# Four hybrid layers on one core: the matmul stream takes a chunk's high part first, and tiles are placed at multiples of 512 bytes

## What is computed

```python
def layer_even(x, norm_g, w_in, w_out):            # layer_odd has the same frame
    h = rmsnorm(x, norm_g)
    qa, ka, va, iq, ik, iw, qb, kb, vb, gate = split_cols(h @ w_in, SPLIT0)
    ...                                             # sparse attention, dilated attention
    return x + (y * jax.nn.silu(gate)) @ w_out

def second_block(x, ...):
    h = rms_norm(x, norm_w[i]); proj = h @ w_in[i]
    o_a = gdn_branch(...)                           # gated delta rule, chunks of 64, triangular inverse
    o_b = rwkv7_branch(...)                         # RWKV-7 recurrence
    o_c = s5_branch(...)                            # complex diagonal scan, then a gelu and a product with glu_w
    branch_proj = einsum('blnc,ncd->blnd', stack([o_a, o_b, o_c]), w_branch[i])
    merged = sum(sigmoid(gate_logits + gate_b) * branch_proj)
    x = x + merged @ w_out[i]
    return rms_norm(x, final_norm_w)
```

## Time and profile before

| | us |
|---|---|
| runs | 2404.01, 2408.6, 2412.79 |
| profiled execution | 2403.41 |
| its span | 2401.6 |
| TensorE matmul busy | 2238.3 (93%) |
| VectorE busy | 1585.6 (66%) |
| ScalarE busy | 1070.5 (45%) |
| mean granted clock | 0.981 |

### The profile page before, as it was taken

The page is one execution under the profiler, slowest core; times in us unless marked ns, Lnnn a source line. Parts: engine busy times, 40 slices in busy tenths (PEclk is TensorE's granted clock), DMA queues, the critical chain, the costliest instruction groups (busy, mean ns, idle before and its releaser), DMA issues.

```text
span 2401.6 us, 35278 instructions
## 1 busy us (share of the span) xinstructions
PE 2238.3 (93%) x14268; PEld 1840.7 (77%) x14268; DVE 1585.6 (66%) x2362; ACT 1070.5 (45%) x1490; POOL 115.2 (5%) x188
## 2 busy tenths in 40 slices
PE   7999889999999999999999989888899989989997
PEld 6889678887878788877777767776677777767876
DVE  5665675558894546659999675665955556567754
ACT  5444565445444655553333653233444323244443
POOL 0000001010001001000000100001010000011000
PEclk9999999999999999999999999999999999989999
DMA  7666338667687449775554734249676333477753
GB/s 232 189 192 203 99 117 298 225 193 247 234 290 283 154 155 334 239 254 195 185 189 152 249 111 155 84 135 338 231 288 217 125 109 114 139 275 237 244 188 124
DMA packets 222594, 481.67 MB, mean 201 GB/s; under 512 B 14880, under 2 KB 51536, under 8 KB 217696
## 3 DMA queue, kind: packets, MB, share of 16 engines
q1 hardware_dynamic: 200112, 372.91, 47.2%
q0 software_dynamic: 22320, 106.51, 12.1%
HBM read 421.97 MB, written 57.40 MB: 200 GB/s over the span
## 4 chain that ended last, share of the span: by engine, by line
PE 72%; DVE 14%; DMA 6%; ACT 4%; issue 3%; POOL 0%; SPq 0%; ACTq 0%; POOLq 0%; DVEq 0%
PE mm_acc L291 59%; DVE mm_lo L208 3%; DMA mm_raw<-in_w_in 2%; ACT mm_hi L201 2%; PE s_bu L2819 1%; PE s_y L2832 1%; DMA rwk_src<-rw_rh 1%; DVE gdn_cv L1829 1%; DMA in_xt<-proj 1%; PE in_turn L374 1%; PE rwk_bank L2343 0%; DMA in_xt<-x 0%; DMA in_xt<-in_x 0%; DMA rw_v<-rwp_ft 0%; DVE s5t_tab L2718 0%
## 5 line engine op out<-in xcount | busy, mean ns | idle before, releaser
L208 DVE TENSOR_TENSOR mm_lo<-mm_raw,mm_hi 128x1024 fp32r<-128x1024 f32 (+4 forms) x672 | 791.9, 1185 | 525.6 <-ACT mm_hi L201 516.3
L201 ACT CAST mm_hi<-mm_raw 128x1024 fp32r<-128x1024 f32 (+4 forms) x672 | 681.8, 1019 | 862.2 <-PE mm_acc L291 827.2
L291 PE MATMUL mm_acc<-mm_hi,mm_aT_hi 128*128 128x512 f32 (+5 forms) x2208 | 880.3, 399 | 40.7 <-DVE mm_lo L208 35.5
L291 PE MATMUL mm_acc<-mm_hi,mm_aT_lo 128*128 128x512 f32 (+5 forms) x2208 | 852.0, 386 | 0.0
L291 PE MATMUL mm_acc<-mm_lo,mm_aT_hi 128*128 128x512 f32 (+5 forms) x2208 | 851.3, 386 | 0.0
L291 PEld LDWEIGHTS mm_acc<-mm_hi,mm_aT_hi 128*128 128x128 f32 x2208 | 421.6, 191 | 134.5 <-DVE mm_lo L208 48.0
L291 PEld LDWEIGHTS mm_acc<-mm_hi,mm_aT_lo 128*128 128x128 f32 x2208 | 420.8, 191 | 77.5
L291 PEld LDWEIGHTS mm_acc<-mm_lo,mm_aT_hi 128*128 128x128 f32 x2208 | 422.0, 191 | 67.5 <-issue 1.0
L291 PE MATMUL mm_acc<-mm_hi,in_yT_hi 128*128 128x512 f32 x256 | 101.7, 397 | 3.0 <-DVE mm_lo L208 3.0
L291 PE MATMUL mm_acc<-mm_hi,in_yT_lo 128*128 128x512 f32 x256 | 100.5, 393 | 0.0
L291 PE MATMUL mm_acc<-mm_lo,in_yT_hi 128*128 128x512 f32 x256 | 100.4, 392 | 0.0
(11 more groups left out here) (635 smaller groups left out, 2155.6 us busy)
## 6 DMA issues: line engine op xcount, KB each, us to landing
mm_raw<-in_w_in SPq DMA_DIRECT2D x384, 512.0 KB, 5.4
mm_raw<-in_w_out SPq DMA_DIRECT2D x96, 512.0 KB, 5.2
mm_raw<-in_w_in SPq DMA_DIRECT2D x72, 464.0 KB, 4.1
mm_raw<-in_w_branch SPq DMA_DIRECT2D x48, 512.0 KB, 5.3
proj<-mm_stage SPq DMA_DIRECT2D x46, 512.0 KB, 3.1
mm_raw<-in_w_in SPq DMA_DIRECT2D x32, 416.0 KB, 4.9
home_tab<-s5t_tab POOLq DMA_DIRECT2D x4, 2048.0 KB, 9.6
s_tab<-home_tab POOLq DMA_DIRECT2D x8, 1024.0 KB, 5.9
```

The source lines that it names most:

```text
L201: self.nc.scalar.copy(self.hi[:, c % RING, :, 0:t.w], self.raw[:, c % RAW, :, 0:t.w]).then_inc(self.hi_done, 1)
L208: self.nc.vector.tensor_tensor(self.lo[:, c % RING, :, 0:t.w], self.raw[:, c % RAW, :, 0:t.w], self.hi[:, c % RING, :, 0:t.w].bitcast(F32) ...
L291: last = nc.tensor.matmul(self.acc[s][m][:, 0:t.w], t.aT[a][:, k, m * P:(m + 1) * P], b[:, c % RING, k - k0, 0:t.w], start=(k == 0 and fir ...
```

## The change

Two edits. The first splits the wait of a chunk: TensorE waits for the high part, issues the 8 matmuls with `mm_hi`, then waits for the low part and issues the 4 matmuls with `mm_lo`. The second changes the allocation: a tile of under 512 bytes for each partition comes from the right end of SBUF, every other one starts at a multiple of 512 bytes. (`n` counts 4 bytes an element.)

```diff
+LINE = 512
...
     def sb(self, name, shape, dt=F32):
-        return self.stack.enter_context(self.nc.sbuf_tensor(f"{self.name}_{name}", shape, dt))
+        n = 4 * int(np.prod(shape[1:]))
+        place = dict(side="right") if n < LINE else dict(align_bytes=LINE)
+        return self.stack.enter_context(self.nc.sbuf_tensor(f"{self.name}_{name}", shape, dt, **place))
...
+            pe.wait_ge(self.hi_done, c + 1)
+            for k in range(k0, k0 + KC):
+                for m in range(MT):
+                    for a in range(2):
+                        nc.tensor.matmul(self.acc[s][m][:, 0:t.w], t.aT[a][:, k, m * P:(m + 1) * P], self.hi[:, c % RING, k - k0, 0:t.w],
+                                         start=(k == 0 and a == 0), stop=False)
             pe.wait_ge(self.lo_done, c + 1)
             for k in range(k0, k0 + KC):
                 for m in range(MT):
-                    for a, b, first, end in ((0, self.hi, True, False), (0, self.lo, False, False), (1, self.hi, False, True)):
-                        last = nc.tensor.matmul(self.acc[s][m][:, 0:t.w], t.aT[a][:, k, m * P:(m + 1) * P],
-                                                b[:, c % RING, k - k0, 0:t.w],
-                                                start=(k == 0 and first), stop=(k == t.KT - 1 and end))
+                    last = nc.tensor.matmul(self.acc[s][m][:, 0:t.w], t.aT[0][:, k, m * P:(m + 1) * P], self.lo[:, c % RING, k - k0, 0:t.w],
+                                            start=False, stop=(k == t.KT - 1))
             last.then_inc(self.used, 1)
```

## The result

| | before | after |
|---|---|---|
| median of six runs, us | 2408.98 (2404.01 to 2412.79) | 2387.4 (2381.28 to 2394.58) |
| ratio | | 0.9909, interval 0.9895 to 0.9923 |
| profiled execution, us | 2403.41 | 2388.49 |
| its span | 2401.6 | 2386.7 |

The kernel became faster by 0.91% (21.9 us by the ratio); the forecast was 25 us and 2383. The profiled execution of before lies 5.6 us under the median of its runs and that of after 1.1 us over its own, so the two spans differ by 14.9 us only; sums over the trace are held against that number. Most of the 5.6 us can be put down to the clock: over 34 executions of the kernel before on one chip, 0.001 more of mean granted clock goes with 2.0 us less, and the profiled one had 0.981 where their mean is 0.979, an estimated 4 us.

A forecast was written before the change was run, and what follows sets the result against it. TensorE was taken as the bound in most stretches (72% of the chain), by instruction count times distance. 16 us (split wait) + 6 (operand places) + 3 (scan) = 25 off 2408.6 gave 2383; eight times in ten 2300 to 2409.

The forecast's parts named there:

- the cap of 8 matmuls: In each late chunk, the saving is at most the 8 matmuls that fit before the low part is needed, 1.82 us.
- the 20 named as a sign: TensorE's waits for `mm_lo` were to fall from 40.4 us to under 20, with `mm_hi` waits at the seams.
- the 14.7 us outside that stretch: Outside 1600 to 1740 us, 15 waits of 18.7 us, less 4 for those over their cap, were to save 14.7.
- the 3 us for the two waits ahead of the load: Between 1600 and 1740 us, only the two waits before the 26.6 us load were to count, 3 us.
- at most some 15 us: Between 1600 and 1740 us, local savings of 13 waits at 1.3 to 1.8 us each, with the cap.
- the upper bound of 30: Largest saving allowed for the split wait, 14.7 + 15 us; the lower bound was 0, all absorbed.
- The 6 us for `in2_yT` and `tail_bT`: In `in2` and the tail, matmuls were to fall to 227.5 ns, saving 2.2 and 3.9, together 6 us.
- The 3 us of the scan: Scan's 12-matmul pieces exceed 2.73 us, perhaps partly from tiles at 288; 3 us taken, bounds 0 and 10.
- The reason given for the 6 us: In dense matmuls, a stationary tile off a multiple of 128 bytes was said to cost about 5.7 ns a matmul.
- The freed gap: Stream matmuls with both operands at 512 lose the whole 14.6 ns gap to 213.3 ns; 91 us, result 2302; 17%.
- The second wait: The mid-chunk wait breaks the stream even when met, adding 74 us over 672 chunks; result 2457; 9%.
- The absorbed case: Freed waits return at the next thing TensorE waits for, and the tail's distance stays; 2404 to 2409; 16%.

## Why the prediction was right, step by step

**Edit 1, forecast 16 us, measured alone 11.6.** The mechanism is as put: the waits outside 1600 to 1740 us fell by 12.8 us (14.7 forecast), with the cap of 8 matmuls seen in the stall at 597 us. The waits for `mm_lo` alone fell to 7.7 us, under the 20 named as a sign; but the new waits for `mm_hi` are not mainly at the seams, 11.0 of their 15.4 us lie between 1600 and 1740. There the fall is 21.7 - 17.2 = 4.5, and the chain there goes over loads and VectorE as in the earlier trace rows:

```profile
1636.71 15.33 DMA mm_raw<-in_w_in
1652.07 1.05 ACT mm_hi L204
1653.21 1.23 DVE mm_lo L211
1654.44 3.48 DVE rwp_pv L2157
...
1664.60 10.69 DMA rw_v<-rwp_ft
```

The terms that were too large are the 14.7 us outside that stretch, where the waits gave 12.8, and the 3 us for the two waits ahead of the load. By the start of the same chunk in both profiles the lead was 12.3 us at 1584 us (times of the profile after), 13.3 at 1629, 15.3 at 1635, 12.8 at 1768 and 11.2 at 1832, then grew to 14.7 in the tail, mostly by edit 2. So over the stretch that was to give 3 us the lead fell by 1.1; with the first edit alone it grew by 0.7 over the same chunks.

Part of such movements is the clock and no wait that turns up again. The step from 12.8 to 11.2 is one chunk, 5.3 us long after and 3.7 before, by the windows view (busy by engine, then granted clock, DMA share, GB/s), first after, then before:

```profile
1786.60:1791.90 5.30, 5.30 (x24) 4.30 (x22) 1.23 (x1) 2.88 (x5) 0.00 (x0) 0.68 0.86 308
```
```profile
1799.40:1803.10 3.70, 3.70 (x24) 3.15 (x22) 0.66 (x1) 2.88 (x5) 0.00 (x0) 1.00 0.93 353
```

TensorE is busy throughout in both, at a granted clock of 0.68 after (partly at the lower level, 1.2 GHz) against 1.00 before. The other way round, the kernel before had 0.92 from 748 to 770 us where after had 1.00, which gave 1.7 us of lead. One pair of traces can't size a term of 2 or 3 us, and the interval of the first edit alone (8 to 15 us) nearly reaches the forecast. One sum of the prediction doesn't come out either: 13 waits at 1.3 us are 16.9 already, so its "at most some 15 us" and the upper bound of 30 were too low; the result doesn't hang on them.

**Edit 2, forecast 6 + 3.** The 6 us for `in2_yT` and `tail_bT` came as worked out: 233.2 to 227.1 over 379 pairs and 233.3 to 227.0 over 668, 2.3 + 4.2 = 6.5 us. That they reached the end is told by the second edit alone, 4 to 12 us by its interval. The 3 us of the scan did not come. A period still lasts 7.67 us (1108.83 to 1116.50, against 1120.51 to 1128.18 in the earlier trace rows):

```profile
1108.83 2.04 PE mm_acc L294 x8
1110.88 0.91 PE mm_acc L299 x4
1111.78 0.81 PE s_y L2839 x8
1112.60 1.93 PE mm_acc L294 x8
1114.53 0.92 PE mm_acc L299 x4
1115.44 1.06 PE s_bu L2826 x4
1116.50 2.04 PE mm_acc L294 x8
```

The excess there is all in the 8 matmuls after a change of work; the 4 low ones take 0.91 us, which is 4 x 0.227. The scan's tiles went from 288 to 0 without any effect on the period: it is not their places, and what is left is the restart after other work. Against it, the 464-wide matmuls of `even` lost 861 x 3.3 ns = 2.8 us, which no step foresaw.

**The sum.** 25 us were forecast and 21.9 came (18.5 to 25.3 by the interval). The terms found since make less: 11.6 for edit 1 and 6.5 for the two operands, less 2.8 in `even`, are some 15 us. The two profiled spans differ by 14.9, by some 19 with the estimated 4 us of the clock. No term accounts for what is then left to 21.9, about the half-width of the intervals (3.3 to 4.1 us). So the sum came nearer than its terms did, and part of that is luck.

**The reason given for the 6 us was wrong.** The prediction held it to be the stationary tile's own place modulo 128. That it gave the right number was luck: the change makes every difference 0, where both rules agree. It would have failed on the first kernel that moved both tiles together (227 instead of 233), or one by 128 (232 instead of 227).

**Rivals.** The freed gap (2302 us) is out: with both operands at 0 the distance is 226.7 ns and not 213.3, nor was it lower at any of the differences tried. The 215.8 ns that the prediction takes there from the Trainium skill (TensorE: Matmul & The Clock Gate, "Back-to-back issue gap") is that section's figure for an isolated matmul, not for a stream with a weight load each, and no piece here came to it. The second wait costs nothing: in the dense pieces the chunk with two waits takes 12 x 226.7 ns. The absorbed case is out, since each edit alone is faster with its interval clear of 1. The 512 KB loads land in 5.0 to 5.3 us (5.2 to 5.4 before) and DMA keeps 6% of the chain; no gain from the places is seen in them.

## What to carry to other kernels

Where a late helper feeds only part of a chunk's matmuls, issue the others first: each wait shrinks by the time of those others at most, and only where TensorE is on the chain. In a dense matmul stream divide the length of a piece by its count and compare pieces: a few ns apiece are invisible in durations and waits. When two operands are streamed together, move them together and then apart before saying which one's place matters.

## What the runs showed of the hardware

The distance of dense 512-wide fp32r matmuls with a weight load each depends on the places of moving and stationary operand in SBUF by their difference modulo 256 bytes, at five of the eight multiples of 32: 226.7 ns at 0, 228.9 to 233.3 at the others, all at the full granted clock (1.00). At 2.4 GHz 226.7 ns are 544 cycles for 512 columns. That the two reads get in each other's way fits this, but no run shows it directly. The Trainium skill (SBUF — State Buffer, "Who interferes with whom") calls TensorE's two read ports independent and says it never waits on anyone; the distances here differ by up to 6.6 ns with the places alone, and the measurement decides.
